# The intra-chunk recurrence levels of an HGRN2 mixer: whole 128x128 products against strips of 32 keys with 32 queries

## The reference, cut to what matters

```python
def step(S, blk):
    qc, kc, vc, gc = blk
    b = jnp.cumsum(gc, axis=2)
    diff = jnp.where(causal, b[:, :, :, None, :] - b[:, :, None, :, :], -jnp.inf)
    decay = jnp.exp(diff)
    att = jnp.einsum('bhtk,bhsk,bhtsk->bhts', qc, kc, decay)
    o = jnp.einsum('bhts,bhsv->bhtv', att, vc) + jnp.einsum('bhtk,bhkv->bhtv', qc * jnp.exp(b), S)
    ...
```

## Time and profile before

| | |
|---|---|
| time, median of 3 runs | 1619.7 us (1615.0 to 1620.96) |
| the profiled execution's own time | 1618.15 us |
| its span | 1616.0 us |
| PE busy | 1557.0 us (96%) |
| PEld busy | 1522.9 us (94%) |
| DVE busy | 1094.1 us (68%) |
| ACT busy | 688.3 us (43%) |
| POOL busy | 42.1 us (3%) |
| mean granted TensorE clock | 0.993 |

### The profile page before, as it was taken

The page is one execution under the profiler, slowest core; times in us unless marked ns, Lnnn a source line. Parts: engine busy times, 40 slices in busy tenths (PEclk is TensorE's granted clock), DMA queues, the critical chain, the costliest instruction groups (busy, mean ns, idle before and its releaser), DMA issues.

```text
span 1616.0 us, 25015 instructions
## 1 busy us (share of the span) xinstructions
PE 1557.0 (96%) x10103; PEld 1522.9 (94%) x10103; DVE 1094.1 (68%) x1991; ACT 688.3 (43%) x1198; POOL 42.1 (3%) x46
## 2 busy tenths in 40 slices
PE   5999999999989989999999999999999999999999
PEld 4999999999778989999999999999999989999998
DVE  5678889764659887788865787886462875443332
ACT  4433334464654466333344633334453266333333
POOL 2000000002100000000000000000000000000000
PEclk8999999999999999999999999999999999999999
DMA  9765656567220245656554565565463344443321
GB/s 327 250 209 169 199 174 218 192 210 228 70 91 27 92 149 166 208 174 198 178 176 136 184 202 188 183 195 170 131 209 124 112 153 160 131 130 114 107 66 39
DMA packets 255681, 260.07 MB, mean 161 GB/s; under 512 B 6625, under 2 KB 253826, under 8 KB 255570
## 3 DMA queue, kind: packets, MB, share of 16 engines
q1 hardware_dynamic: 250528, 253.25, 48.5%
q0 software_dynamic: 928, 2.44, 0.6%
q10 hardware_dynamic: 4114, 2.84, 0.6%
HBM read 255.88 MB, written 2.62 MB: 160 GB/s over the span
## 4 chain that ended last, share of the span: by engine, by line
PE 82%; DVE 10%; ACT 4%; issue 3%; POOL 1%; DMA 1%; ACTq 0%; DVEq 0%; POOLq 0%
PE bank L440 24%; PE bank L441 24%; PE bank L442 24%; DVE PARTS L1088 1%; DVE WL L409 1%; ACT WH L395 1%; PE bank L462 1%; PE bank L1614 1%; PE bank L463 1%; PE bank L464 1%; DVE X L1154 1%; PE bank L1911 1%; DVE HL L1117 1%; DVE SUMS L1419 1%; POOL WL L409 1%
## 5 line engine op out<-in xcount | busy, mean ns | idle before, releaser
L409 DVE TENSOR_TENSOR WL<-RAW,WH 128x1024 fp32r<-128x1024 f32 (+1 forms) x335 | 398.2, 1193 | 419.0 <-ACT WH L395 418.0
L395 ACT ACTIVATE WH<-RAW 128x1024 fp32r<-128x1024 f32 (+1 forms) x344 | 357.5, 1043 | 605.5 <-PE bank L442 593.4
L440 PE MATMUL bank<-HH,WH 128*128 128x384 f32 x1664 | 564.1, 339 | 8.0 <-DVE WL L409 3.5
L442 PE MATMUL bank<-HH,WL 128*128 128x384 f32 x1664 | 560.3, 337 | 0.0
L441 PE MATMUL bank<-HL,WH 128*128 128x384 f32 x1664 | 560.2, 337 | 0.0
L440 PEld LDWEIGHTS bank<-HH,WH 128*128 128x128 f32 x1664 | 313.9, 189 | 9.8 <-issue 3.9
L441 PEld LDWEIGHTS bank<-HL,WH 128*128 128x128 f32 x1664 | 313.7, 189 | 0.0
L442 PEld LDWEIGHTS bank<-HH,WL 128*128 128x128 f32 x1664 | 313.5, 188 | 0.0
L440 PE MATMUL bank<-AH,WH 128*128 128x384 f32 x704 | 237.0, 337 | 0.0
L441 PE MATMUL bank<-AL,WH 128*128 128x384 f32 x704 | 236.6, 336 | 0.0
L442 PE MATMUL bank<-AH,WL 128*128 128x384 f32 x704 | 236.6, 336 | 0.0
(11 more groups left out here) (244 smaller groups left out, 1470.3 us busy)
## 6 DMA issues: line engine op xcount, KB each, us to landing
RAW<-in_ffn_w_in SPq DMA_DIRECT2D x88, 1024.0 KB, 5.2
RAW<-in_mod_w SPq DMA_DIRECT2D x72, 1024.0 KB, 5.0
RAW<-in_ffn_w_out SPq DMA_DIRECT2D x32, 1024.0 KB, 5.2
RAW<-in_ab_w_in SPq DMA_DIRECT2D x16, 1024.0 KB, 5.9
RAW<-in_ffn_w_out SPq DMA_DIRECT2D x16, 768.0 KB, 4.4
RAW<-in_cv_w_in SPq DMA_DIRECT2D x12, 1024.0 KB, 5.2
...
```

The lines of the kernel that those rows point to most:

```text
L395: e.activation(WH[:, (2 * m + b) % 4, 0:nk, :], RAW[:, p, 0:nk, b * P:(b + 1) * P], ACT.Copy).then_inc(half_hi, 1)
L409: e.tensor_tensor(WL[:, k, 0:nk, :], RAW[:, p, 0:nk, b * P:(b + 1) * P], WH[:, k, 0:nk, :].bitcast(F32), ALU.subtract).then_inc(half_ready, 1)
L440: e.matmul(out, WH[:, k, kk, :], xh(kk), start=(first and kk == 0), stop=False)
L442: mm = e.matmul(out, WL[:, k, kk, :], xh(kk), start=False, stop=(last and kk == nk - 1))
```

## The change

Each unit's 128x128 product is replaced. In the diagonal and at levels 0 to 4 (INNER = 5) keys and queries can only meet within a block of BLK = 32 tokens; so PE forms, for each unit, four products of 32 keys with the 32 queries of the same block, the j-th into partitions 32j to 32j+31, and the twelve units stand side by side as 12 x 32 columns of one bank. Level 5 takes the 32 keys of a block with the 32 queries of the neighbouring block, level 6 takes 64 keys with the 64 queries of the other half. The bank changes from level to level (`level_bank`). All full results of levels 5 and 6 are wanted, so they need no mask.

DVE's masked copies go from three of 512 elements at each of seven levels to one of 384 at each of five, into a compact tile ATTD. ATT, which the product with V reads, is put together from it: four copies on POOL for the blocks on the diagonal (32 partitions each), four on ACT from level 5's bank (at level 6), four on ACT from the banks of level 6 (ahead of `proj(31)`'s SiLU). PE waits for all twelve ahead of the first product with V. On DVE the order within a level is now: three key products (which wait for the join), three query products (which wait for PE), the masked copy, three totals, the weight split. The mask shrinks from 7 x 128 to 5 x 32 columns.

```diff
@@ -114,10 +116,10 @@
 
 def constants():
 
-    s = np.arange(P)[:, None]
-    t = np.arange(P)[None, :]
-    masks = np.zeros((P, LEVELS, P), np.int32)
-    for lv in range(LEVELS):
+    s = np.arange(P)[:, None] % BLK
+    t = np.arange(BLK)[None, :]
+    masks = np.zeros((P, INNER, BLK), np.int32)
+    for lv in range(INNER):
         b = 1 << lv
         masks[:, lv] = (s // (2 * b) == t // (2 * b)) & (s // b != t // b)
     q = np.arange(P) % GRID_W
...
@@ -204,7 +206,7 @@
         ACC, ROOT, RSTD = (SUMS[:, i * NT:(i + 1) * NT] for i in range(3))
         IDENT = sb("IDENT", [P, P])
         ONES = sb("ONES", [P, P])
-        LMASK = sb("LMASK", [P, LEVELS, P], I32)
+        LMASK = sb("LMASK", [P, LEVELS * P], I32)[:, 0:INNER * BLK].rearrange("p (l t) -> p l t", l=INNER)
         WINDOW = sb("WINDOW", [P, GRID_W])
         PAR = sb("PAR", [P, NT])
         COND = sb("COND", [P, KD, 32])
...
@@ -265,6 +267,7 @@
 
         QB = BK
         ATT = mix(2 * W15, UNITS, P)
+        ATTD = mix(3 * W15, UNITS, BLK)
         ST = mix(3 * W15 + 384, 8, P)
         OUTM = mix(AT0 + 2 * W15, KD, NT)
         KS = G.rearrange("p h n -> p (h n)").rearrange("p (u t) -> p u t", u=UNITS)
...
@@ -526,6 +530,10 @@
             step = z.offset - a.offset + (b if right is None else right) - left
             return bass.AP(tensor=a.tensor, offset=a.offset + at + left, ap=[a.ap[0], [2 * b, blocks], [step, 2], [1, b]])
 
+        def level_bank(lv):
+
+            return bank[(0, 1, 2, 0, 1, 2, 0)[lv]]
+
         def two_totals(t, other, at, blocks, b, left, right, n):
 
             a, z = t.rearrange("p h n -> p (h n)"), other.rearrange("p h n -> p (h n)")
...
@@ -629,6 +637,11 @@
                     bias_load(h + 2)
             pool.wait_ge(pv_done, 24)
             pool.dma_start(ST, state_hgrn[0, 0].rearrange("w h k v -> k (w h) v")).then_inc(state_landed, 16)
+            pool.wait_ge(v_stored, 16)
+            pool.wait_ge(lvl_out, INNER)
+            for j in range(4):
+                at = slice(BLK * j, BLK * j + BLK)
+                pool.tensor_copy(ATT[at, :, at], ATTD[at]).then_inc(att_near, 1)
 
             for s in range(2, 6):
                 half_low(f"in{s}")
...
@@ -922,6 +935,7 @@
                     for j in range(3):
                         if lv:
                             act.wait_ge(lvl_k, 3 * (lv - 1) + j + 1)
+                            act.wait_ge(lvl_mm, 3 * (lv - 1) + j + 1)
                         act.activation(KJ[:, 512 * j:512 * j + 512].rearrange("p (m w i) -> p m w i", w=2, i=b),
                                        two_halves(KFW, KBW, 512 * j, 256 // b, b), ACT.Copy).then_inc(k_joined, 1)
 
...
@@ -929,12 +943,22 @@
                 for lv in range(LEVELS):
                     join(lv)
                     if lv == 0:
+                        act.wait_ge(diag_mm, 3)
+                        act.activation(ATTD, level_bank(2)[:, 0:UNITS * BLK].rearrange("p (u t) -> p u t", u=UNITS),
+                                       ACT.Copy).then_inc(diag_out, 1)
+                    if lv == 6:
                         act.wait_ge(v_stored, 16)
-                        for j in range(3):
-                            act.wait_ge(diag_mm, j + 1)
-                            act.activation(ATT[:, 4 * j:4 * j + 4, :].rearrange("p u t -> p (u t)"), bank[j][:],
-                                           ACT.Copy).then_inc(diag_out, 1)
+                        B = level_bank(5)[:, 0:UNITS * BLK].rearrange("p (u t) -> p u t", u=UNITS)
+                        for j in range(4):
+                            rows, cols = slice(BLK * j, BLK * j + BLK), slice(BLK * (j ^ 1), BLK * (j ^ 1) + BLK)
+                            act.activation(ATT[rows, :, cols], B[rows], ACT.Copy).then_inc(att_far, 1)
                     proj(24 + lv)
+                act.wait_ge(lvl_mm, 3 * LEVELS)
+                for c in range(2):
+                    B = bank[c][:, 0:384].rearrange("p (u t) -> p u t", t=64)
+                    for j in range(2):
+                        rows, cols = slice(64 * j, 64 * j + 64), slice(64 * (j ^ 1), 64 * (j ^ 1) + 64)
+                        act.activation(ATT[rows, 6 * c:6 * c + 6, cols], B[rows], ACT.Copy).then_inc(att_far, 1)
                 proj(31)
                 for h in range(HEADS_A):
                     act.wait_ge(k_turned, h + 1)
...
@@ -1368,28 +1392,28 @@
                 for lv in range(LEVELS):
                     b = 1 << lv
                     for j in range(3):
-                        dve.wait_ge(lvl_mm, 3 * lv + j + 1)
-                        if lv == 0:
-                            dve.wait_ge(diag_out, j + 1)
-                        else:
-                            dve.wait_ge(lvl_out, 3 * (lv - 1) + j + 1)
-                            dve.wait_ge(lvl_t, 3 * (lv - 1) + j + 1)
-                        mask = LMASK[:, lv:lv + 1, :].broadcast_to([P, 4, P])
-                        dve.copy_predicated(ATT[:, 4 * j:4 * j + 4, :], mask,
-                                            bank[j][:].rearrange("p (u t) -> p u t", u=4)).then_inc(lvl_out, 1)
+                        dve.wait_ge(k_joined, 3 * lv + j + 1)
                         if lv == 0:
                             dve.wait_ge(q_gated, j + 1)
+                        else:
+                            dve.wait_ge(lvl_t, 3 * (lv - 1) + j + 1)
                         k = two_halves(KFW, KBW, 512 * j, 256 // b, b)
                         dve.tensor_tensor(k, k, two_totals(FF, FB, 512 * j, 256 // b, b, b, 0, b),
                                           ALU.mult).then_inc(lvl_k, 1)
+                    for j in range(3):
+                        dve.wait_ge(lvl_mm, 3 * lv + j + 1)
                         q = two_halves(QB, QF, 512 * j, 256 // b, b)
                         dve.tensor_tensor(q, q, two_totals(FB, FF, 512 * j, 256 // b, b, b, 0, b),
                                           ALU.mult).then_inc(lvl_q, 1)
-                        if j:
-                            totals(lv, j - 1)
+                    if lv < INNER:
+                        dve.wait_ge(lvl_out, lv) if lv else dve.wait_ge(diag_out, 1)
+                        dve.copy_predicated(ATTD, LMASK[:, lv:lv + 1, :].broadcast_to([P, UNITS, BLK]),
+                                            level_bank(lv)[:, 0:UNITS * BLK].rearrange("p (u t) -> p u t", u=UNITS)) \
+                            .then_inc(lvl_out, 1)
+                    for j in range(3):
+                        totals(lv, j)
                     if 1 <= lv <= 4:
                         split_dve(dve, f"in{s}", 14 + (lv - 1) // 2, 8)[(lv - 1) % 2]()
-                    totals(lv, 2)
                 dve.wait_ge(state_landed, 16)
                 dve.wait_ge(lvl_t, 3 * LEVELS)
                 for h in range(HEADS_A):
...
@@ -1890,27 +1914,46 @@
 
                 pe.wait_ge(proj_out, 24)
                 pe.wait_ge(s_exp, 24)
+                def blocks(out, keys, queries):
+
+                    for j in range(4):
+                        mm = pe.matmul(out[BLK * j:BLK * j + BLK], keys(BLK * j), queries(j), start=True, stop=True)
+                    return mm
+
                 for j in range(3):
                     pe.wait_ge(ks_done, j + 1)
                     for u in range(4 * j, 4 * j + 4):
-                        mm = pe.matmul(bank[j][:, (u % 4) * P:(u % 4 + 1) * P], KS[:, u, :], unit(QF, u),
-                                       start=True, stop=True)
+                        mm = blocks(level_bank(2)[:, BLK * u:BLK * u + BLK], lambda at: KS[:, u, at:at + BLK],
+                                    lambda i: unit(QF, u)[:, BLK * i:BLK * i + BLK])
                     mm.then_inc(diag_mm, 1)
                 proj(24)
+                qb, qf = (t.rearrange("p h n -> p (h n)") for t in (QB, QF))
                 for lv in range(LEVELS):
                     b = 1 << lv
+                    if lv == 2:
+                        pe.wait_ge(diag_out, 1)
+                    if lv >= 3:
+                        pe.wait_ge(lvl_out, min(lv - 2, 4))
+                    if lv == 6:
+                        pe.wait_ge(lvl_out, INNER)
                     for j in range(3):
-                        if lv == 0:
-                            pe.wait_ge(diag_out, j + 1)
-                            pe.wait_ge(q_gated, j + 1)
-                        else:
-                            pe.wait_ge(lvl_out, 3 * (lv - 1) + j + 1)
-                            pe.wait_ge(lvl_q, 3 * (lv - 1) + j + 1)
+                        pe.wait_ge(q_gated, j + 1) if lv == 0 else pe.wait_ge(lvl_q, 3 * (lv - 1) + j + 1)
                         pe.wait_ge(k_joined, 3 * lv + j + 1)
                         for u in range(4 * j, 4 * j + 4):
-                            mm = pe.matmul(bank[j][:, (u % 4) * P:(u % 4 + 1) * P],
-                                           KJ[:, P * u:P * u + P],
-                                           two_halves(QB, QF, P * u, 64 // b, b), start=True, stop=True)
```

(16 more changed lines are left out.)

5 lines of the change are left out of this document (4 added, 1 removed).

## The result

The changed kernel took 1605.35 us (median of four runs, 1602.07 to 1605.75) against 1618.62 us (four runs, the three shown above and one of 1617.54): a ratio of 0.9914, 95% interval 0.9899 to 0.9929. That is 0.86% or 13.3 us faster; the forecast was 1603.0, in a range from 1598 to 1612.

What follows compares the result with a forecast made beforehand. DVE and PE were both taken as full in the even sub-layer's recurrence. Keys turned at 521.3 instead of 538.0 gives 16.7 us, less 1.2 for clock: 15.5 off 1618.15 is 1602.7, or 1604.2 from the median; stated 1603.0, range 1598 to 1612.

Steps and rivals of the forecast that it cites:

- the moment to move: PE starting to turn the keys at 538.00 us; each microsecond taken off it should come off the end.
- The schedule: Worked times for PE and DVE through levels 0 to 6 of the stage, ending with the SiLU at 521.3 us.
- The masked copy: DVE: five copies of 384 elements replace 21 of 0.63 us; each taken as 0.49 us, 2.4 us together.
- 33 ns for a group of four: PE's strips: four small products side by side take 33 ns, so 0.8 us a level in place of 2.68.
- the fold: PE's nearest existing rows, moving 16 columns: eight records start within 0.07 us, 35 ns a group.
- The floor as a rival: PE's strip records cost 29.5 ns whatever their columns, 2.8 us a level; gain 8.8 us, 1609.4 us; chance 0.20.
- one drop to half clock in the stage: PE's new idle before level 3 was assumed to bring one clock drop, costing 1.2 us.
- The low-clock rival: Strip bursts between waits leave PE at 1.2 GHz through the stage: 13.3 us later, 1631.4 us; chance 0.06.
- POOL's copies: Four diagonal copies on POOL, at most 0.94 us each, starting about 511 us, after the fifth masked copy.
- The cover of 7 us: Slack between POOL's diagonal copies, starting about 511, and PE's need of them at 522.4 us.
- ACT's copies: Strip copies on ACT, 0.4 to 0.47 us each; the last four, 1.6 us, have about 1 us of cover.
- Level 6: PE's last level, as two 64x64 products a unit at 56 ns a pair: 1.35 us.

Runs made afterwards that it cites:

- e1: The kernel before with only DVE's order changed, key products ahead of the masked copies and waiting for the join, strips not used: ratio 0.9984 to the kernel before.
- e9: The changed kernel plus eight unread 128x128 products (six at level 6) once behind each projection on PE: 1612.69 us against 1605.49 beside it.
- e0: The changed kernel run once more, unedited, against the kernel before: median 1605.53 us against 1617.95, ratio 0.9921.
- e11: The changed kernel run again, unedited, as base for three runs beside it: 1605.49 us against 1617.44 for the kernel before, ratio 0.992.
- e2: The changed kernel with every 32x32 product issued three times (diagonal and levels 0 to 5; level 6 once): 1641.55 us, ratio 1.0147 to the kernel before.
- e4: The changed kernel with key products also waiting for the level's PE products again: ratio 0.994 to the kernel before.
- e6: The changed kernel with POOL's four diagonal copies of ATT moved to ACT: ratio 0.9921 to the kernel before.
- e7: The changed kernel plus eight (level 6: six) unread 128x128 products a level on PE, ahead of each third of the strips: 1618.89 us.

## Why the prediction was right, and where it was not

**The bound.** PE and DVE were both full, and the moment to move was that of the first turned key. That held: after it the two profiles take the same 1078 us, to 0.1. e1 and e9 show that DVE's side alone does not give it: by the medians the order alone 2.0 us, all of DVE's relief with the short diagonal 4.7 or a little more, with PE's shorter levels 12. Whether PE's side alone would give it, no run tried.

**The schedule.** In the first profile level 0's first query product was worked out at 481.7 and started at 481.56; DVE's levels at 488.3, 495.2, 501.3, 507.0 and 512.6 started at 488.23, 495.07, 501.21, 506.98 and 512.58; level 3's strips, after idling, at 497.7, measured 497.65; the end of the stage, before the clock's share, at 521.3, measured 522.04. That the absolute times agree is partly luck: the head was worked out from a profile in which DVE's first product came at 471.15 and PE was at half clock; in the first profile after, it came 1.7 us later and PE was at full clock, and the two made up. In e0 every one of these starts is 0.6 to 0.7 us behind the forecast, in e11 1.5 to 1.6. What was right in all three are the lengths: from one level's key products to the next the forecast has 6.9, 6.1, 5.7 and 5.6 us from level 1 on, and the three profiles 6.82 to 6.84, 6.14 to 6.16, 5.77 to 5.80 and 5.59 to 5.61. The masked copy was taken at 0.49 us and held DVE for 0.48.

**The strips.** 33 ns for a group of four, 0.8 us a level, was taken from the fold; 96 records in 1.07 us, of which the last takes 0.2, are 36 ns, and the level is 1.00 us to the start of the projection. The floor as a rival fell for bursts of this length, by the strips' rows above and by PE's 3 us to spare. The Trainium skill's floor of about 25 ns a matmul ("TensorE: Matmul & The Clock Gate", Back-to-back issue gap), which the prediction weighed, is not there in four column strips side by side: 9 ns a record, 18 for a product of two. But the rival had a true core that the prediction didn't see: e2's 28 ns a record in a long run comes from supply.

**The clock.** The prediction took off 1.2 us for one drop to half clock in the stage. PE idled for 1.67 us ahead of 497.65 (2.2 foreseen), and in the first profile and in e0 no drop followed; in e11 one fell at 501.2 and cost 0.5 us at most (41.00 against 40.49), and in e4 one cost nothing, since PE had idle time and DVE's row set the pace. So this term was too large. It hid that the schedule without it was 0.7 us short, at the end of the stage. Where the clock did cost time is the head: 1.3 us for 3.4 us at half clock, 1.9 for 6.8. The low-clock rival was far off in the change, but e2 is of that kind: PE stalled for 15 us in the stage and had six such stretches. (The sixteen stretches that the prediction gives this rival do not follow from its sum: 551.3 less 475.0 is 22 of them.)

**Mis-sized or missing terms.** POOL's copies were taken at 0.94 us at most, by its bias addition, and took 8.34 us together: the first came into DVE's row of products and stood until about 517. The cover of 7 us ended as 3. DVE's level 6 beside them took 4.9 us instead of the 3.9 foreseen. Both were covered: e6 shows that nothing was lost. ACT's copies took 0.5 us each (taken at 0.4 to 0.47), with 1.12 us of the cover left. Level 6 was 1.62 us instead of 1.35. The switches of form, 0.27 us a round trip in e7, had no term of their own.

**Time and median.** The profiled run was forecast at 1602.7 and took 1602.07. The median, 1605.4 to 1605.5 in all three sets, lies 3 us above it: 1.3 to 1.5 of that is the stretch at half clock near 1268, and 1.3 to 1.9 the one in the head, which e0 and e11 show and the first profile doesn't. The prediction placed its number between profile and median, 1603.0, and so was 2.4 us low. Its gain of 15.5 us fits the pair of profiles (16), which differ in the clock as well; by the medians the gain was 13.3, 12.4 and 11.9 us, around the lower edge of the 12.5 to 18 that the prediction gave its forecast. Its remark that less than 0.5% can't be told from none was too cautious: the intervals are 0.15% to either side, and e1's 0.16% is clear of none.
